# Whole 2 MB weight transfers in the middle turns of an expert loop, with the last turn written out on TensorE and SyncE

## The reference, cut to what matters

```python
def expert_block(args):
    tok, e = args
    hdn = x_pad[tok] @ w1[e] + b1[e]          # 1024 -> 2048
    glu, lin = hdn[:, :D_FF], hdn[:, D_FF:]
    ...
    act = glu * jax.nn.sigmoid(SWIGLU_ALPHA * glu) * (lin + 1.0)
    return act @ w2[e] + b2[e]                # 1024 -> 1024
```

## Time and profile before

| | |
|---|---|
| median of 3 runs | 1285.0 (1284.16 to 1285.87) |
| the profiled execution | 1284.71 |
| its span (first to last instruction) | 1282.9, so 1.8 lie around it |
| TensorE matmul busy | 95% of the span |
| mean granted TensorE clock | 0.99 |
| read from HBM | 460.56 MB |

### The profile page before, as it was taken

One profiled execution on the slowest core, in us unless ns is written; L12 is line 12 of the kernel. 1 busy time (PEld: TensorE's weight loads), 2 busy tenths in 40 slices (PEclk: granted clock), 3 DMA queues, 4 the chain that ended last, 5 costly groups with the idle time before them and its releaser, 6 DMA issues.

```text
span 1282.9 us, 19007 instructions
## 1 busy us (share of the span) xinstructions
PE 1217.3 (95%) x8094; PEld 671.6 (52%) x8094; DVE 399.2 (31%) x874; ACT 186.0 (15%) x372; POOL 131.0 (10%) x122
## 2 busy tenths in 40 slices
PE   9999999999999999999999998989898989989896
PEld 8888789999964344434444333434243333424341
DVE  3859694575432121121111212021111202120213
ACT  1442621110031011101000010101010010101011
POOL 1000046788100000000000000000000000000001
PEclk9999999999999999999999999999999989999998
DMA  7745327458899999999999999999999999999996
GB/s 273 219 144 168 133 100 310 147 202 300 333 388 422 410 428 427 424 425 428 426 422 420 427 428 423 426 429 423 427 428 429 422 430 428 429 422 430 428 426 248
DMA packets 54560, 463.37 MB, mean 361 GB/s; under 512 B 12320, under 2 KB 14272, under 8 KB 19456
## 3 DMA queue, kind: packets, MB, share of 16 engines
q1 hardware_dynamic: 48576, 459.99, 87.6%
q10 hardware_dynamic: 5920, 2.45, 0.7%
HBM read 460.56 MB, written 1.87 MB: 360 GB/s over the span
## 4 chain that ended last, share of the span: by engine, by line
PE 57%; DMA 23%; SPq 3%; DVE 2%; POOL 1%; issue 1%; ACT 1%; POOLq 0%; DVEq 0%
PE ps L1228 26%; DMA ring<-expert_w 12%; DMA mix<-expert_w 11%; PE ps L712 8%; PE ps L1248 7%; PE ps L1135 4%; PE ps L1117 4%; SPq L592 3%; PE ps L1030 2%; PE ps L746 1%; DMA mix<-stream_w 1%; PE ps L1237 1%; PE ps L735 1%; PE ps L1221 1%; POOL ring L652 1%
## 5 line engine op out<-in xcount | busy, mean ns | idle before, releaser
L1228 PE MATMUL ps<-ring,mix 128*64 128x512 f32 x1504 | 338.1, 593 | 10.4 <-DMA ring<-expert_w 10.3
L1228 PEld LDWEIGHTS ps<-ring,mix 128*64 128x64 f32 x1504 | 104.5, 137 | 201.3 <-issue 178.3
L1248 PE MATMUL ps<-ring,mix 128*64 128x512 f32 x752 | 171.9, 595 | 16.5 <-DMA ring<-expert_w 16.5
L1228 PE MATMUL ps<-mix 128*64 128x512 f32 x544 | 130.9, 624 | 13.2 <-DMA mix<-expert_w 13.2
L735 PE MATMUL ps<-mix 128*128 128x256 f32 x624 | 136.8, 380 | 0.0
L2262 DVE TENSOR_SCALAR mix<-ps 128x512 f32<-128x512 f32 x32 | 22.1, 692 | 354.4 <-PE ps L1228 354.4
L735 PEld LDWEIGHTS ps<-mix 128*128 128x128 f32 x624 | 117.9, 190 | 17.1 <-issue 1.3
L1248 PEld LDWEIGHTS ps<-ring,mix 128*64 128x64 f32 x752 | 51.8, 137 | 120.0 <-issue 85.0
L674 POOL TENSOR_TENSOR mix<-mix 128x1024 f32<-128x1024 f32 (+1 forms) x2 | 3.4, 1700 | 948.7 <-ACT mix L1669 948.7
L712 PE MATMUL ps<-mix 128*128 128x128 f32 x792 | 97.0, 276 | 0.3 <-POOL mix L652 0.3
L712 PEld LDWEIGHTS ps<-mix 128*128 128x128 f32 x792 | 92.1, 192 | 1.1 <-POOL mix L652 0.5
(11 more groups left out here) (301 smaller groups left out, 972.7 us busy)
## 6 DMA issues: line engine op xcount, KB each, us to landing
ring<-expert_w SPq DMA_DIRECT2D x106, 2048.0 KB, 30.4
mix<-expert_w SPq DMA_DIRECT2D x39, 2048.0 KB, 27.6
ring<-expert_w SPq DMA_DIRECT2D x70, 1024.0 KB, 25.5
mix<-stream_w SPq DMA_DIRECT2D x42, 1024.0 KB, 5.1
mix<-expert_w SPq DMA_DIRECT2D x15, 1024.0 KB, 14.3
mix<-expert_w SPq DMA_DIRECT2D x18, 512.0 KB, 24.9
mix<-stream_w SPq DMA_DIRECT2D x8, 512.0 KB, 4.3
mix<-first_w SPq DMA_DIRECT2D x4, 512.0 KB, 4.9
```

The costliest lines, as they stand in the source:

```text
L1228: ins = mm(PS[64 * a:64 * a + 64, bank + g, :], XE[j][:, c, 64 * a:64 * a + 64], w[2 * a + g], start=start, stop=(c == KD - 1), skip_group ...
L1248: ins = mm(PS[64 * a:64 * a + 64, bank + h, :], HT[:, c // 4, c % 4, 64 * a:64 * a + 64], w[2 * h + a], start=(c == 0), stop=(c == KF - 1) ...
```

## The change

Only turn 0 and the closing turn (`CLOSING` = 7) get steps 20 to 22 in halves and step 23 in three parts. In turns 1 to 6 all 24 steps are one transfer each. On SyncE the loop ends before turn 7, which is written out behind it. On TensorE turns 4 to 6 are a loop with a constant bound, turn 7 is written out, and only then `rounds` is read; further rounds stand in a loop of their own under an `If`.

```diff
+CLOSING = NPAIR // PB - 1
...
                     singly = isinstance(turn, int) and turn == 0
+                    closing_turn = isinstance(turn, int) and turn == CLOSING
...
-                    elif n in PARTED:
+                    elif n in PARTED and (singly or closing_turn):
                         for k, event in enumerate((PARTED[n], f"steps_in{(n - AHEAD) % SLOTS}")):
...
-                    elif n < PB * EC // STEPS - 1:
+                    elif n < PB * EC // STEPS - 1 or not closing_turn:
                         load_steps(n, pair + n // (EC // STEPS), (n - AHEAD) % SLOTS)
...
-            with sp.Fori(STATIC, NPAIR // PB) as q:
+            with sp.Fori(STATIC, CLOSING) as q:
                 load_turn(q, q * PB)
+            load_turn(CLOSING, CLOSING * PB)
             sp.wait_ge(E("rounds_ready"), 1)
...
-                    if m in PARTED and n % STEPS == 0:
-                        pe.wait_ge(E(PARTED[m]), 16 * turn + (32 if m == 22 else 48))
+                    if m in PARTED and n % STEPS == 0 and isinstance(turn, int) and turn in (0, CLOSING):
+                        pe.wait_ge(E(PARTED[m]), (16 if turn else 0) + (32 if m == 22 else 48))
...
-                    if n == PB * EC - 1:
-                        pe.wait_ge(E("last_in"), 16 * turn + 16)
+                    if n == PB * EC - 1 and isinstance(turn, int) and turn == CLOSING:
+                        pe.wait_ge(E("last_in"), 16)
...
-                        if h == 1 and j * EC + 2 * KD + c == PB * EC - 1:
-                            pe.wait_ge(E("last_right_in"), 16 * turn + 16)
+                        if (h == 1 and j * EC + 2 * KD + c == PB * EC - 1 and isinstance(turn, int)
+                                and turn == CLOSING):
+                            pe.wait_ge(E("last_right_in"), 16)
...
             for turn in range(STATIC):
                 for j in range(PB):
                     pair(turn, j)
+            with pe.Fori(STATIC, CLOSING) as turn:
+                for j in range(PB):
+                    pair(turn, j)
+            for j in range(PB):
+                pair(CLOSING, j)
             pe.wait_ge(E("rounds_ready"), 1)
             rounds = pe.value_load(NR[0:1, 0:1], min_val=1, max_val=ROUNDS)
-            with pe.Fori(STATIC, rounds * (NPAIR // PB)) as turn:
-                for j in range(PB):
-                    pair(turn, j)
+            with pe.If(rounds > 1):
+                with pe.Fori(NPAIR // PB, rounds * (NPAIR // PB)) as turn:
+                    for j in range(PB):
+                        pair(turn, j)
             pe.wait_ge(E("ys_left"), rounds * NPAIR)
```

## The result

The changed kernel takes 1289.46 us (median of 6 runs, 1288.56 to 1291.3), the kernel before 1285.16 beside it: a ratio of 1.0036, with a 95% interval of 1.0026 to 1.0047. That is 4.3 us slower, where 0.2 slower was forecast and the range ended at 1288.4. The profiled execution after took 1288.56, with a span of 1286.8 against 1282.9.

The account below looks back on a forecast made before the run. The prediction took the DMA engines' time for the bytes as the bound, with TensorE's last scatter and VectorE's statistics on the path at the end; -2.3 + 0 + 0.3 + 0.1 + 2.1 = +0.2 gave 1285.2 us, range 1282.2 to 1288.4.

Parts of the forecast that it names:

- part 5: TensorE's jump over the further rounds before the last scatter: a fetch with nothing in front of it, +2.1 us.
- the sum: Whole kernel: -2.3 + 0 + 0.3 + 0.1 + 2.1 = +0.2 us, added to the median of 1285.0.
- rival C: Between last `down` and scatter: long jump stall makes it slower, deciding from 4.5 us, clock included; chance 0.17.
- Part 1: Expert weight transfers, turns 1 to 6: whole steps make 30 transfers fewer in a full queue, -2.3 us.
- Rival D: Expert weight transfers: a transfer costs more than the spacing shows, no miss, -5.6 us to 1279.4; chance 0.06.
- The sentence that the slices are full from about 385 on: Profile slices of 32 us: from the twelfth on, the 16 DMA engines are at 9 tenths or more.
- Part 2: TensorE's start on whole steps, turns 1 to 6: its waits spread over the four steps, price 0.
- Part 3: Turn 7 written out on TensorE: five instruction blocks more to fetch in the DMA-bound stretch, +0.3 us (0 to 0.4).
- Part 4: Reading `rounds` behind the last `down`, before the scatter: +0.1 us (0 to 0.3).

## Why the prediction was wrong

**The step that failed is part 5, and with it the sum.** Its mechanism was right: the branch over five blocks misses, stalls TensorE's sequencer between the last `down` and the scatter, and delays the statistics. Its size was not. I took 2.1 from a 16 KB transfer. Measured were 3.54 to 3.75 where one fetch lies in the stall, and 4.96 and 4.98 in the two profiles with two. The lower clock, which I left out of the sum, came as well and cost 1.3, after an idle time of 3.60. So the term was 4.5 to 4.7, by the end's rows and by the kernel before with the skip alone, and 6.0 to 6.3 in the two profiles with two fetches (the end is 20.6 and 20.9 behind the last release, for 14.6). This is the prediction's rival C, a stall with clock of 4.5 or more, at 0.17. Its own sign, the weight loads' idle time before the scatter of 4 and more, came true with 4.47. C said that against it stood the empty queues; they were nearly empty (a DMA share of 0.14 from 1268.0 to 1272.4), and the stall came all the same. Weighing a fetch by a data transfer was the weak step: the branch's 3.54 to 4.98 had no row before the change.

Part 1 was right. The 30 transfers fewer were to give 2.3. The kernel with nothing else gives 2.7 in time (1.4 to 3.9 by its interval of 0.997 to 0.9989), and the spacing of the turns came out at 117.48 there and 117.51 in the changed kernel. Rival D, which asks for 5.6, falls. The sentence that the slices are full from about 385 on misreads the row by one slice, since the twelfth begins at 353; nothing hangs on it.

Part 2 was right: the waits spread over the steps, 1.3 at a turn's start, and nothing was lost. Step 0 of turn 7 came 0.75 earlier than before (1154.70 for 1155.45), not later.

Part 3 was too low: 0.3 with a bound of 0.4, where the profiles have 0.1 to 1.6, 1.0 on average (in time 0.6, between -0.4 and 1.9 by the interval). The failing step was to read the price from turn 4 of one profile; the eight written-out profiles show how much it varies.

Part 4 was right: 0.1, and nothing measurable.

One term was missing: the wait for GpSimd at 320 us, 1.2 longer (1.9 for 0.7) in the changed kernel. In the first profile TensorE's matmuls on L735 start at 329.10 before, those on L738 at 330.67 after, so 1.6 later. It fits with turn 5 beginning at the same time in spite of the faster turns. No run changes this wait alone, so its price is argued.

The terms as measured are -2.7, +1.0, +4.6 and +1.2, together +4.1, beside the 4.3 of the comparison. That this fits so closely is partly luck: the 4.6 holds for one fetch in the stall, how many of the timed runs had two is not known, and the same comparison a second time gave 3.6. The branch was covered by nothing; the gain was real, and it was outweighed by a cost at the one place where TensorE's sequencer is on the path.

The Trainium skill's rule that I weighed, in "Runtime: NRT & Kernel Launch", section "Instruction fetch mechanics", that a taken branch out of the current window waits for its target, agrees with the branches of 3.54 to 4.98 over 2.6 blocks and more, and of 0.35 over one wait. Of its two figures the window of two pages fits these, and not the 2048 instructions as something that is held ahead: 660 were already too far. For branches backwards the rule as it stands does not agree with the trace: the loop's branches go back over five blocks and took 76 to 252 ns, with no fetch at all after 930. There the measurement decides.

## What to carry to other kernels

Look at every forward branch over a large body on the engine that ends the kernel: skipping code isn't free. It should belong where a wait covers it, or the common path should fall through; neither was tried here. A loop whose body the engine holds was cheaper than the same turn written out, by 1.0 on average in the profiles; where only one turn is to be loaded differently, the issuing engine can be written out and can raise the semaphores for the others. Fewer and larger transfers in a full queue are worth only what the spacing of their landings shows, here 0.1 us for each step of 2 MB.

## What the runs showed of the hardware that was not expected

A taken branch to code 660 or 1300 instructions on took 3.54 to 3.75 us in four kernels, with one fetch in it, and 4.96 to 4.98 in two more profiles of one of them, with two. All weight transfers had landed by then. Over one wait it took 0.35. Such a stall also costs the clock: with TensorE idle for 3.60 the granted clock fell to 0.50 within the next matmuls, and 16 of them took 5.35 instead of 3.76; when it had worked the clock was 1.00, and 15 took 3.97. A turn written out 800 us later went with a wait of 1.0 to 1.2 us in an unchanged stretch instead of 0.5 to 0.7, and with a skipped loop behind that turn of 1.8 to 1.9, the same within 0.1 in each repetition of a program.
